# A transformer trunk on one core: some expert chunks loaded in three transfers instead of one

## What is computed

```python
def swiglu(h, w_gate, w_up, w_down):
    return (jax.nn.silu(h @ w_gate) * (h @ w_up)) @ w_down

def moe_swiglu(h, w_router, b_router, w_gate, w_up, w_down):
    ...
    for e in range(N_EXPERTS):
        y = y + combine[:, e:e + 1].astype(h.dtype) * swiglu(ht, w_gate[e], w_up[e], w_down[e])
    return y.reshape(B, S, D)
```

## Time and profile before

| | us |
|---|---|
| Runs | 1305.44, 1312.6, 1307.8 (median 1307.8) |
| The profiled execution, its own time | 1312.05 |
| Its span, first to last instruction | 1310.2 |
| TensorE busy | 1247.2 (95% of the span) |
| VectorE busy | 338.7 (26%) |
| ScalarE busy | 287.6 (22%) |
| DMA queue q1 (SP's loads and stores) | 419.09 MB, 79.5% of 16 engines' time |
| Mean granted TensorE clock | 0.984 |

### The profile page before, as it was taken

The page is one execution under the profiler, slowest core; times in us unless marked ns, Lnnn a source line. Parts: engine busy times, 40 slices in busy tenths (PEclk is TensorE's granted clock), DMA queues, the critical chain, the costliest instruction groups (busy, mean ns, idle before and its releaser), DMA issues.

```text
span 1310.2 us, 27064 instructions
## 1 busy us (share of the span) xinstructions
PE 1247.2 (95%) x12436; PEld 721.1 (55%) x12437; DVE 338.7 (26%) x696; ACT 287.6 (22%) x494; POOL 39.0 (3%) x48
## 2 busy tenths in 40 slices
PE   7988999999997989999999999999998999998896
PEld 6866788888855774333663343663342564333363
DVE  5877555445356431001000011000010000001001
ACT  5575552434247510000000000000000000000000
POOL 1012000000002200000000000000000000000000
PEclk9999999999997979999999999999999999999999
DMA  9632455464353298999999999999999999999994
GB/s 347 226 129 97 133 189 193 124 220 146 108 173 129 113 374 322 409 408 426 425 423 425 427 425 426 424 424 425 425 427 426 426 425 425 425 425 426 426 424 165
DMA packets 64107, 423.62 MB, mean 323 GB/s; under 512 B 5760, under 2 KB 13686, under 8 KB 39414
## 3 DMA queue, kind: packets, MB, share of 16 engines
q1 hardware_dynamic: 62780, 419.09, 79.5%
q0 software_dynamic: 992, 2.69, 0.6%
q10 hardware_dynamic: 218, 0.08, 0.0%
HBM read 420.77 MB, written 1.07 MB: 322 GB/s over the span
## 4 chain that ended last, share of the span: by engine, by line
PE 82%; DMA 10%; DVE 4%; ACT 3%; issue 1%; SPq 0%; DVEq 0%; ACTq 0%
PE PS L2151 32%; PE PS L2180 16%; DMA places_raw<-in_w_down_o_dram 9%; PE PS L1642 7%; PE PS L1646 7%; PE PS L1643 7%; PE PS L1965 2%; PE PS L2188 2%; PE PS L2090 1%; DVE w_r L921 1%; PE PS L2073 1%; ACT w_r L476 1%; PE PS L1761 1%; PE PS L1744 1%; PE PS L1743 1%
## 5 line engine op out<-in xcount | busy, mean ns | idle before, releaser
L2151 PE MATMUL PS<-places_raw,xe 128*32 128x512 f32 (+1 forms) x3760 | 362.4, 540 | 10.6 <-DMA places_raw<-in_w_up_o_dram 10.6
L2151 PEld LDWEIGHTS PS<-places_raw,xe 128*32 128x32 f32 x3760 | 119.5, 110 | 240.5 <-issue 218.8
L1642 PE MATMUL PS<-w_r,a_hi 128*128 128x512 f32 (+4 forms) x384 | 144.7, 381 | 5.5 <-DVE a_lo L950 4.6
L1643 PE MATMUL PS<-w_r,a_lo 128*128 128x512 f32 (+4 forms) x384 | 141.9, 373 | 0.0
L921 DVE TENSOR_TENSOR w_r<-raw,w_r 128x2048 fp32r<-128x2048 f32 (+4 forms) x61 | 129.1, 2144 | 43.1 <-ACT w_r L476 43.0
L2151 PE MATMUL PS<-places,xe 128*32 128x512 f32 (+1 forms) x1360 | 133.3, 540 | 4.0 <-DMA places<-in_w_up_o_dram 4.0
L476 ACT ACTIVATE w_r<-raw 128x2048 fp32r<-128x2048 f32 (+4 forms) x61 | 106.7, 1801 | 14.9 <-PE PS L1646 13.1
L2180 PE MATMUL PS<-places_raw,e_l 128*32 128x256 f32 x1848 | 106.4, 380 | 2.2 <-DMA places_raw<-in_w_down_o_dram 2.2
L1646 PE MATMUL PS<-w_r,a_hi 128*128 128x512 f32 (+4 forms) x384 | 98.6, 374 | 0.0
L2151 PEld LDWEIGHTS PS<-places,xe 128*32 128x32 f32 x1360 | 43.3, 110 | 87.7 <-issue 80.2
L1496 DVE TENSOR_TENSOR e_l<-PS,e_l 128x896 f32<-128x896 f32 x12 | 12.3, 1085 | 278.2 <-PE PS L2151 278.2
(11 more groups left out here) (302 smaller groups left out, 1017.4 us busy)
## 6 DMA issues: line engine op xcount, KB each, us to landing
places_raw<-in_w_gate_o_dram SPq DMA_DIRECT2D x48, 1792.0 KB, 27.0
places_raw<-in_w_up_o_dram SPq DMA_DIRECT2D x46, 1792.0 KB, 31.8
places_raw<-in_w_down_o_dram SPq DMA_DIRECT2D x44, 1792.0 KB, 37.7
places<-in_w_down_o_dram SPq DMA_DIRECT2D x19, 1792.0 KB, 36.3
places<-in_w_up_o_dram SPq DMA_DIRECT2D x18, 1792.0 KB, 32.2
places<-in_w_gate_o_dram SPq DMA_DIRECT2D x16, 1792.0 KB, 30.5
raw<-in_w_in_e_dram SPq DMA_DIRECT2D x12, 1024.0 KB, 9.9
raw<-in_w_down_e_dram SPq DMA_DIRECT2D x11, 1024.0 KB, 4.9
```

The source lines that it names most:

```text
L1642: nc.tensor.matmul(dst, xh, wh, start=first, stop=False)
L1643: nc.tensor.matmul(dst, xl, wh, start=False, stop=False)
L2151: ins = nc.tensor.matmul(PS[g * Q:(g + 1) * Q, bank + c0 // NT, 0:c], xe[:, at, x0:x0 + Q], w[:, g * QW + c0:g * QW + c0 + c], start=at == ...
```

## The change

Of the chunks from 16 (SG) on, those with n mod 12 = 6 are loaded in three transfers, of partitions 0 to 111, 112 to 119 and 120 to 127, one after the other from SP and with the same bytes to the same place. All three add 16 to the semaphore of the place, and `landed` counts them: 48 for such a chunk, 16 for others. There are 15 of these chunks, 18, 30, ... 186.

```diff
+PARTED = 12
+FEW = 8
...
+        def parted(n):
+
+            return n >= SG and n % PARTED == PARTED // 2
+
         def landed(n):
-            return ex_full[n % E_PLACES], 16 * (n // E_PLACES + 1)
+            return ex_full[n % E_PLACES], sum(16 + 32 * parted(m) for m in range(n % E_PLACES, n + 1, E_PLACES))
...
                 if n == LAST:
                     sp.dma_start(dst[:, :, 0:LAST_AT], src[:, :, 0:LAST_AT]).then_inc(landed(n)[0], 16)
                     sp.dma_start(dst[:, :, LAST_AT:EW], src[:, :, LAST_AT:EW]).then_inc(sem("last_full"), 16)
+                elif parted(n):
+                    for lo, hi in ((0, P - 2 * FEW), (P - 2 * FEW, P - FEW), (P - FEW, P)):
+                        sp.dma_start(dst[lo:hi], src[lo:hi]).then_inc(landed(n)[0], 16)
                 else:
                     sp.dma_start(dst, src).then_inc(landed(n)[0], 16)
```

## The result

The changed kernel takes 1514.91 us (median of four runs, 1507.67 to 1522.12), the kernel before 1310.2 us beside it: a ratio of 1.156 (95% interval 1.151 to 1.161). It is 205 us slower, 13.6 us for each of the 15 cut chunks. I had forecast 1305.3 us, and a range of 1300 to 1328.

The account below looks back on a forecast made before the run. The pace of the transfer engines, through the last chunk's landing, was taken to set the end. Added costs of 0 and a 2.5 us gain from shifted rows took the 1307.8 us median to 1305.3, range 1300 to 1328.

Parts of the forecast that it names:

- The reading of the kernel before: Expert stream: the last transfer's landing at 1297.86 sets the end; TensorE waits 19.7 us for chunks, with 12.3 us behind it.
- dips at every twelfth chunk: Sign in the expert stream's rate, 425 GB/s if the prediction was right, that small transfers collide at the destination.
- The zero prices for issues, completions and counts: SP and TensorE in the stream: 30 more issues at 0.333 us, 30 more completions and larger wait counts cost nothing.
- the 112 rows are seven per engine: Large transfer of each cut chunk: every engine does one row less, at 0.54 us a row.
- the lead of 12.8 us: Stream's tail, 1278 to 1294: eight engines finish 8 to 14 us before the other eight, 12.8 on average.
- The collision rival: Small transfers' rows queue at neighbouring partitions: 1.6 us more each, 30 times, 48 us; 1351 us, chance 0.18.
- the range 0 to 1.6: Extra us per small transfer from collision at the destination; 0 taken, gain gone beyond 0.16.
- The gain itself: Stream's end: shifting rows to the early eight engines gains 0 to 4.7 us, 2.5 taken; perfect balance bounds it at 6.4.
- the case that the small transfers run on the early eight engines: Cut chunks' extra rows go to engines done first; late ones end 8.1 us sooner; 1305.3 us, chance 0.54.
- the late eight: Wrong half rival: small transfers run on the engines that finish last, ending 8.1 us later; 1315.9 us, chance 0.15.

Follow-up runs that it names:

- four cuts by rows: 15 chunks cut as 112 + 8 + 8 (changed kernel), 112 + 16, 64 + 64, or 96 + 32 rows: 1514.91, 1495.87, 1493.02, 1513.32 us.

## Why the prediction was wrong

The reading of the kernel before held: the end is set by the last landing, TensorE follows it, and after the change the loss shows up as waits for chunks. The sign that I had named for the collision, dips at every twelfth chunk, is there, and the last landing comes at 1493.4 instead of 1297.86. The zero prices for issues, completions and counts held (the cut by columns: ratio 0.9998).

**The step that failed** is "the 112 rows are seven per engine; on these alone every engine does one row less than before". I counted rows and took it that a row takes an engine 0.54 us wherever it goes. On these alone the kernel is 166 us slower. The 0.54 us hold in transfers over all 128 partitions. With each of the four cuts by rows all 16 run at about half pace (226 to 244 GB/s from 586 to 602), and not for the chunk's own time but, as I read the windows, until the last of them is through, which the lead of 12.8 us, the very thing that I had read from the tail, stretches to 40 us.

**The collision rival** had the right mechanism with the wrong place and size. I put it on the two small transfers only, 1.6 us each and 48 us in all. By the one stretch shown they measured about what I had set (3.8 us a cut chunk against 3.2), but the large transfer, which I had not put under the same rule, costs three times as much (166 / 15 = 11 us a cut chunk). And I took zero of the range 0 to 1.6 because the steady stream showed no limit on the receiving side. That was no evidence: every transfer in it goes to all 128 partitions, so a limit on a part of them could not show.

The Trainium skill ("SBUF — State Buffer", Door 1) has the rule that spoke against the change, and I quoted it and gave it little weight: 16 ports, each for two blocks of four partitions. The runs agree as far as direction goes: 64 rows at a time run at 238 of 425. That rule of the Trainium skill by itself would make a chunk of 64 + 64 rows 4.3 us longer by my estimate, and 12.3 were measured.

**The gain itself** could not have come either. I gave 0.54 to the case that the small transfers run on the early eight engines, and 0.15 to the late eight. It is neither: six and two, as the tails and the small packets read. By my estimate the two late ones would end 15 x 0.54 = 8.1 us later and set the end, so that even without any collision the change would have cost some 8 us. Of what the Trainium skill says in the section of "DMA: Bandwidth & Descriptors" on why a DMA increments its semaphore by 16, eight engines for eight rows agrees with the packet counts (8 + 8 for each small transfer); which eight by number the trace doesn't name.

What stays open is which engine writes which partitions, in a full transfer and in a cut one: no trace says it. So a collision on the receiving side is the reading that fits all runs, and not a thing that one of them shows directly. The packet records come nearest. Near the end of the changed kernel's stream three engines are left; between 1466.9 and 1469.5 two of them take 1.13 to 1.14 us for each row at the same time, while the third goes on at 0.54: two are slow together, and not every engine. That in the full stream all 16 are slowed, those in ordinary chunks too, would follow if the rows of a cut chunk fall on what the others are writing; and that the lead counts twice would follow from it. Both are argued, not shown; and why some engines of the kernel before get ahead of the others at all no run tests.

## What to carry to other kernels

Where the transfer engines are the limit, keep every load on all 128 partitions, and if it must be cut, cut along the columns: in three transfers that was free here, while a cut by rows cost 12 to 14 us for a chunk of 4.3. A balance of rows per engine says nothing until it is known what the engines write at the same time; a steady stream that shows no limit says nothing about a pattern that is not in it. Before shifting load between engines that the profile doesn't name, measure with one small kernel which of them a transfer of that shape uses.

## What the runs showed of the hardware

- A stretch in which a chunk is cut by rows runs at 197 to 238 instead of 425 GB/s in the windows shown, with all engines busy. For small transfers the partitions written decide, not the rows read (1347.91 us into partitions 64 to 127, 1310.07 into 0 to 63).
- Two engines can be slow together, at 1.13 us a row instead of 0.54, while a third keeps its pace beside them (changed kernel, 1466.9 to 1469.5).
- The length of such a stretch grows along the stream, 12, 24, 32, 40 us, and is 15 to 18 us, drain included, when the engines are brought together first. It fits the cut chunk at half pace plus about twice the distance between the first and the last engine.
- Small transfers of eight rows end with eight completion packets, and run on eight engines, six of the early and two of the late ones.
- Left to itself, a stream on 16 engines in equal shares drifts apart by 14 us over 800 us; bringing the engines together at four places costs less than the drift does when a bad transfer follows.
